# Encoder layer with attention: maxima issued by ScalarE, merged transfers, and a later store of the recurrence's outputs

## The reference, cut to what matters

```python
xn = rms_norm(x, norm_mix)
q, k, v, u, g_attn, g_ssm = jnp.split(xn @ w_in, SPLIT_POINTS, axis=-1)
q = apply_axial_rope(rms_norm(q.reshape(bsz, l, 16, 64), q_norm), cos, sin)
k = apply_axial_rope(rms_norm(k.reshape(bsz, l, 4, 64), k_norm), cos, sin)
attn_out = gqa_attention(q, k, v) @ w_attn_proj      # softmax(q k / 8) v, a kv head for 4 q heads
y = gelu(s5_bidirectional(u, ...))                   # a linear recurrence in both directions
ssm_out = (y @ w_glu_a) * sigmoid(y @ w_glu_b)
x = x + (sigmoid(g_attn) * attn_out + sigmoid(g_ssm) * ssm_out) @ w_out
x = x + square(relu(rms_norm(x, norm_mlp) @ w_ff1)) @ w_ff2
```

## Time and profile before

| what | value |
|---|---|
| time, median of three runs | 2325.09 us (2324.87 to 2328.51) |
| time of the profiled execution | 2325.24 us |
| its span in the trace | 2323.5 us |
| PE busy | 98% of the span |
| VectorE, ScalarE, GpSimd busy | 78%, 51%, 58% |
| TensorE clock granted, mean | 1.00 |

### The profile page before, as it was taken

One profiled execution on the slowest core, in us unless ns is written; L12 is line 12 of the kernel. 1 busy time (PEld: TensorE's weight loads), 2 busy tenths in 40 slices (PEclk: granted clock), 3 DMA queues, 4 the chain that ended last, 5 costly groups with the idle time before them and its releaser, 6 DMA issues.

```text
span 2323.5 us, 43966 instructions
## 1 busy us (share of the span) xinstructions
PE 2287.0 (98%) x14871; PEld 2000.0 (86%) x14871; DVE 1809.7 (78%) x2613; ACT 1192.4 (51%) x1980; POOL 1339.1 (58%) x1113
## 2 busy tenths in 40 slices
PE   8999999999989999999999999999999999999999
PEld 6888888888756666688888889999999999999999
DVE  6888578989878777867676698888888967777776
ACT  7556121121367777844444456555557465555563
POOL 0002864646457777744444446777777877667765
PEclk9999999999999999999999999999999999999999
DMA  5333344443333121165566654333333532222222
GB/s 195 114 125 119 116 122 110 116 123 108 109 89 101 47 60 37 39 205 177 185 201 200 212 176 136 97 97 97 97 98 106 191 128 73 73 73 73 73 73 91
DMA packets 173145, 271.01 MB, mean 117 GB/s; under 512 B 36529, under 2 KB 91057, under 8 KB 172849
## 3 DMA queue, kind: packets, MB, share of 16 engines
q1 hardware_dynamic: 172400, 268.62, 37.2%
q10 hardware_dynamic: 576, 0.27, 0.0%
HBM read 201.13 MB, written 57.67 MB: 111 GB/s over the span
## 4 chain that ended last, share of the span: by engine, by line
PE 89%; DVE 3%; SPq 3%; DMA 2%; ACT 2%; issue 1%; POOL 1%; ACTq 0%; DVEq 0%; POOLq 0%
PE banks L65 9%; PE banks L67 9%; PE banks L66 9%; PE banks L3237 6%; PE banks L3239 6%; PE banks L3240 6%; PE banks L3213 6%; PE banks L3215 6%; PE banks L3216 6%; PE p_acc L65 3%; PE p_acc L66 3%; PE p_acc L67 3%; PE banks L2095 3%; PE banks L2096 3%; PE banks L2064 2%; PE banks L2043 1%
## 5 line engine op out<-in xcount | busy, mean ns | idle before, releaser
L2707 POOL TENSOR_TENSOR t_wlo<-f_sums,t_whi 128x512 fp32r<-128x512 f32 x256 | 360.4, 1410 | 156.7 <-ACT t_whi L2738 156.7
L2995 DVE TENSOR_TENSOR f_x<-banks,f_x 128x384 f32<-128x384 f32 x448 | 245.1, 553 | 94.8 <-PE banks L3240 94.4
L1892 POOL TENSOR_TENSOR a_plo<-a_p 128x512 f16<-128x512 f32 x236 | 248.0, 1059 | 101.4 <-ACT a_p L1938 96.9
L2693 POOL TENSOR_TENSOR t_wlo<-t_wraw,t_whi 128x1024 fp32r<-128x1024 f32 x67 | 164.6, 2457 | 218.8 <-ACT t_whi L2723 218.8
L1938 ACT ACTIVATE a_p<-banks,s_scales 128x512 f32<-128x512 f32 x320 | 248.4, 778 | 82.2 <-PE banks L2096 56.9
L2738 ACT ACTIVATE t_whi<-f_sums 128x512 fp32r<-128x512 f32 x256 | 161.7, 632 | 230.9 <-PE banks L3240 147.1
L3213 PE MATMUL banks<-block,t_whi 128*128 128x384 f32 x720 | 241.7, 336 | 2.6 <-ACT stage L2852 1.5
L3216 PE MATMUL banks<-block,t_wlo 128*128 128x384 f32 x720 | 240.6, 334 | 0.0
L3215 PE MATMUL banks<-block,t_whi 128*128 128x384 f32 x704 | 235.3, 334 | 0.0
L1971 DVE TENSOR_REDUCE stage<-banks 128x1 f16<-128x1024 f32 (+1 forms) x184 | 191.0, 1058 | 43.9 <-PE banks L2064 42.9
L3237 PE MATMUL banks<-block,t_whi 128*128 128x384 f32 x608 | 203.4, 334 | 1.8 <-DVE f_x L2995 1.8
(11 more groups left out here) (428 smaller groups left out, 6840.0 us busy)
## 6 DMA issues: line engine op xcount, KB each, us to landing
t_wraw<-w_tail_t SPq DMA_DIRECT2D x136, 512.0 KB, 4.0
a_quotient<-w_tail_t SPq DMA_DIRECT2D x64, 512.0 KB, 3.8
w_raw<-w_in_t SPq DMA_DIRECT2D x31, 512.0 KB, 3.8
proj_scratch<-s_gate SPq DMA_DIRECT2D x48, 256.0 KB, 2.1
t_graw<-proj_scratch SPq DMA_DIRECT2D x24, 512.0 KB, 3.7
block<-roped_scratch SPq DMA_DIRECT2D x146, 64.0 KB, 2.2
p_sw<-p_qn SPq DMA_DIRECT2D x60, 128.0 KB, 2.1
mix_scratch<-a_quotient SPq DMA_DIRECT2D x48, 128.0 KB, 2.4
```

Of the source, the lines that this page charges most:

```text
L1892: pool.tensor_tensor(p_lo[s][:], p32[s][:], p_hi[s], ALU.subtract).then_inc(plo_pool, 1)
L2707: pool.tensor_tensor(weights_of(t, ring_lo[t % 4]), source(t), f32(weights_of(t, ring_hi[t % 4])), ALU.subtract).then_inc(lo_pool.sem, 1)
```

## The change

1. `place_max` goes from SP to ScalarE, right behind the first exponential of a unit, and places the maxima of the next unit. SP's unit begins with the wait for the scores. PE waits for the maxima between the two score matmuls of the unit's first step, and for the queries of the unit two ahead before the first matmul of its maxima.
2. `roped_scratch` is laid out as `[head, half, 64, tokens]` and no longer `[half, head, 64, tokens]`. The query loads are two DMAs for a unit and no longer three: high and low half as 128 rows into `q1`, and the high half into `q2`. The first keys are loaded by one DMA for each head, whose source is broadcast over the two halves of `k1`, in place of two DMAs for all heads asked for. The stores of `r_hi` and `r_lo` stay one DMA each, with a DRAM side of `[2, 64, 512]`.
3. The store of a pair's outputs is one DMA of 128 rows with a DRAM side of `[2, 64, 512]`, and no longer two of 64 rows; so too in the tail.
4. The stores of the recurrence's last outputs move from A's iterations g 0 and 2 to B's first four iterations, g 0 and 3. The first loads from `mix_scratch` for the next stage move from B's iterations 0 and 1 to B's iteration 4.

```diff
@@ -173,14 +173,14 @@
-        for rows in (0, HEAD):
-            sp.dma_start(self.k1[rows:rows + HEAD, h0:h1, tok],
-                         roped[0, NQ + h0:NQ + h1, :, tok].rearrange("h d n -> d h n")
+        for h in range(h0, h1):
+            sp.dma_start(self.k1[:, h, tok],
+                         roped[NQ + h, 0, :, tok].unsqueeze(0).broadcast_to([2, HEAD, tok.stop - tok.start])
                          ).then_inc(landed, 16)
...
         sp.dma_start(self.k2[0:HEAD, h0:h1, tok],
-                     roped[1, NQ + h0:NQ + h1, :, tok].rearrange("h d n -> d h n")).then_inc(self.k_in[n], 16)
+                     roped[NQ + h0:NQ + h1, 1, :, tok].rearrange("h d n -> d h n")).then_inc(self.k_in[n], 16)
@@ -198,10 +198,9 @@
         tok = bass.ds(blk * BLK, BLK)
-        hi, lo = roped[0][head][:, tok], roped[1][head][:, tok]
-        sp.dma_start(self.q1[kv][0:HEAD], hi).then_inc(self.q_in[kv], 16)
-        sp.dma_start(self.q1[kv][HEAD:P], lo).then_inc(self.q_in[kv], 16)
-        sp.dma_start(self.q2[kv][0:HEAD], hi).then_inc(self.q_in[kv], 16)
+        both = roped[head].rearrange("t d n -> (t d) n")
+        sp.dma_start(self.q1[kv], both[:, tok]).then_inc(self.q_in[kv], 16)
+        sp.dma_start(self.q2[kv][0:HEAD], both[0:HEAD, tok]).then_inc(self.q_in[kv], 16)
@@ -559,9 +558,7 @@
                 head = 4 * i + (2 * (t // NBLK) - (4 if k < 0 else 0))
-                return bass.ds(head * HEAD, P), cols(t % NBLK)
-
-            rows_of = lambda l: roped[l].rearrange("h d n -> (h d) n")
+                return bass.ds(head, 2), cols(t % NBLK)
@@ -577,11 +574,11 @@
                     if has(i, k, behind, own):
-                        rows, tok = place(i, k)
+                        heads, tok = place(i, k)
                         sp.wait_ge(hi_ready, 6 * i + (k + 1))
-                        sp.dma_start(rows_of(0)[rows, tok], r_hi[:, k % 2]).then_inc(hi_out[k % 2], 16)
+                        sp.dma_start(roped[heads, 0, :, tok], r_hi[:, k % 2]).then_inc(hi_out[k % 2], 16)
                         sp.wait_ge(lo_ready, 6 * i + (k + 1))
-                        sp.dma_start(rows_of(1)[rows, tok], r_lo[:, k % 2]).then_inc(lo_out[k % 2], 16)
+                        sp.dma_start(roped[heads, 1, :, tok], r_lo[:, k % 2]).then_inc(lo_out[k % 2], 16)
                 if behind and not own:
@@ -1639,12 +1636,12 @@
-                pe.wait_ge(mid.k_head_in, 32)
+                pe.wait_ge(mid.k_head_in, 16)
                 pe.wait_ge(resp_ready, BATCHES)
...
             def first_max(u_):
-                pe.wait_ge(mid.q_in[u_], 48)
+                pe.wait_ge(mid.q_in[u_], 32)
                 for j in range(4):
@@ -1656,7 +1653,7 @@
             outputs(Batch(None, BATCHES - 1), range(BATCH // 2))
-            pe.wait_ge(mid.k_first_in[0], 32)
+            pe.wait_ge(mid.k_first_in[0], 16 * (NKV - 1))
             first_max(1)
@@ -1804,9 +1801,8 @@
                 sp.wait_ge(moved, pair + 2)
-                for half in range(2):
-                    sp.dma_start(mix[head + NKV * half][:, bass.ds(blk * BLK, BLK)],
-                                 o[t][half * HEAD:(half + 1) * HEAD]).then_inc(stored[t], 16)
+                sp.dma_start(mix[bass.ds(head, 2, NKV), :, bass.ds(blk * BLK, BLK)],
+                             o[t][:]).then_inc(stored[t], 16)
@@ -1815,8 +1811,6 @@
-                if g % 2 == 0:
-                    store_outputs(sp, mix_y, last_y, slice(GROUPS - BATCH, GROUPS), st.y, (2 * g + kv,))
                 if g == 1:
@@ -1825,16 +1819,21 @@
-            def last_stage(g, kv):
-
-                if g == 0 and kv == 0:
+            def outputs_out(g, kv):
+
+                if g in (0, 3):
+                    store_outputs(sp, mix_y, last_y, slice(GROUPS - BATCH, GROUPS), st.y, (kv + (4 if g else 0),))
+
+            def last_stage(kv):
+
+                if kv == 0:
                     sp.wait_ge(pv_done, QKP + B.s0)
...
                     for s in range(2):
-                        sp.wait_ge(stored[s], 32 * (NQ // 4))
-                if g == 0 or kv < 2:
-                    fore.load_first(sp, mix_t, kv if g == 0 else 4 + kv)
+                        sp.wait_ge(stored[s], 16 * (NQ // 4))
+                for c in (kv, 4 + kv)[:2 if kv < 2 else 1]:
+                    fore.load_first(sp, mix_t, c)
             for sq in SEQS:
@@ -1844,9 +1843,6 @@
                         for kv in range(NKV):
-                            u = sq.u0 + it * 4 + kv
-                            if next_seq(sq, last, kv):
-                                mid.place_max(sp, u + 2, (kv + 2) % 4)
                             sp.wait_ge(scored, sq.s0 + sq.n * (it * 4 + kv + 1))
@@ -1862,7 +1858,9 @@
                             elif bi == 0 and isinstance(g, int):
-                                last_stage(g, kv)
+                                outputs_out(g, kv)
+                            elif bi == 1 and isinstance(g, int) and g == 0:
+                                last_stage(kv)
@@ -1924,7 +1922,7 @@
                 if not isinstance(before, int) or before:
-                    act.wait_ge(stored[t], 32 * before)
+                    act.wait_ge(stored[t], 16 * before)
                 act.activation(o[t][:], ps[:, O_BANK + 1], ACT.Copy, scale=mid.v_unscale[:, t:t + 1]).then_inc(moved, 1)
@@ -1937,6 +1935,10 @@
                                            scale=mid.score_scale).then_inc(exp_done, 1)
+                            first_of_all = sq is A and isinstance(it, int) and it == 0 and kv == 0
+                            last_of_all = sq is B and last and kv == NKV - 1
+                            if kt == 0 and not first_of_all and not last_of_all:
+                                mid.place_max(act, it * 4 + (sq.u0 + kv + 1), (kv + 1) % NKV)
                             i = v_part(V_SPLIT, sq, it, kv, kt)
@@ -2077,12 +2079,9 @@
-                        pe.wait_ge(nmax_in[kv], n_of(kv) * 16)
-                        pe.wait_ge(q_in[kv], n_of(kv) * 48)
+                        pe.wait_ge(q_in[kv], n_of(kv) * 32)
                         if sq_ahead is not sq and sq_ahead:
-                            pe.wait_ge(k_first_in[1], 32 * NKV)
-                        if sq_ahead:
-                            pe.wait_ge(q_in[s_ahead], n_of(kv + 2) * 48)
+                            pe.wait_ge(k_first_in[1], 16 * NKV)
                         for kt in range(sq.n):
@@ -2093,6 +2092,8 @@
                             pe.matmul(out, k1[:, kv, keys], q1[kv][:], start=True, stop=False)
+                            if kt == 0:
+                                pe.wait_ge(nmax_in[kv], n_of(kv) * 16)
                             pe.matmul(out, k2[:, kv, keys], q2[kv][:], start=False,
@@ -2110,6 +2111,8 @@
                             if sq_ahead:
+                                if kt == 0:
+                                    pe.wait_ge(q_in[s_ahead], n_of(kv + 2) * 32)
                                 for part in range(sq_ahead.n // sq.n):
@@ -2500,10 +2503,9 @@
                 sp.dma_start(ones[:], ones_d).then_inc(const_in, 16)
-                for half in range(2):
-                    sp.dma_start(mix[0:8].rearrange("t p n -> (t p) n").rearrange("(h d) n -> h d n", d=HEAD)
-                                 [NQ - 1 - NKV * (1 - half)][:, TOK - BLK:TOK],
-                                 fore.o[t_last][half * HEAD:(half + 1) * HEAD]).then_inc(st.attention[t_last], 16)
+                sp.dma_start(mix[0:8].rearrange("t p n -> (t p) n").rearrange("(h d) n -> h d n", d=HEAD)
+                             [bass.ds(NQ - 1 - NKV, 2, NKV), :, TOK - BLK:TOK],
+                             fore.o[t_last][:]).then_inc(st.attention[t_last], 16)
@@ -2620,7 +2622,7 @@
                     for s in range(2):
-                        sp.wait_ge(st.attention[s], 32 * (NQ * NBLK // 4))
+                        sp.wait_ge(st.attention[s], 16 * (NQ * NBLK // 4))
                     mix_chunk(b + 1, 0)
@@ -2764,7 +2766,7 @@
                         act.wait_ge(fore.turned, LAST_PAIR + 3)
-                        act.wait_ge(st.attention[t_last], 32 * (LAST_PAIR // 2))
+                        act.wait_ge(st.attention[t_last], 16 * (LAST_PAIR // 2))
                         act.activation(fore.o[t_last], ps[:, LAST_BANK], ACT.Copy,
@@ -3245,7 +3247,7 @@
     proj = scratch("proj_scratch", [PROJ_T, P, TOK])
-    roped = nc.dram_tensor("roped_scratch", [2, NQ + NKV, HEAD, TOK], F16).ap()
+    roped = nc.dram_tensor("roped_scratch", [NQ + NKV, 2, HEAD, TOK], F16).ap()
     mix = scratch("mix_scratch", [12, P, TOK])
```

## The result

The changed kernel takes 2373.66 us (median of four runs, 2371.75 to 2374.79), the kernel before on the same chip 2325.89: the ratio is 1.0203, with an interval of 1.0185 to 1.0220. The forecast was 2370, with 2338 to 2404 as its range. The span of the profiled execution is 2373.0 us, 49.5 more than before.

The account below looks back on a forecast made before the run. PE, busy 98% of the span, bounds the kernel; its waits for queries in A could be won. From 2325.24: -15.3 +2.0 +0.8 +0.5 +2.5 +27 (first projection) +27 (A) +1 (tail) = 2371, stated as 2370, range 2338 to 2404.

Parts of the forecast that it names:

- A: Attention of sequence A (512 keys): 27 us of new waits for queries, against 15.3 us gained, with small costs on top.
- The narrow transfers: Roped stores, first key loads, pair stores: an outermost count of 2 confines each to the same two DMA engines.
- Rival 2: All merged transfers: a count of 2 doesn't narrow them, so only the first part's gain remains, 2313; chance 0.13 with rival 4.
- Rival 3: Pair stores in A: at 8.2 us each fills a pair of units, seven more waits of about 3.5 us, 2395; chance 0.12.
- First projection: First projection: narrow roped stores slow VectorE until PE loses 27 us (18 to 38).
- the period of a tile: First projection: stores, swap and weights on two engines take 7.0 us a tile (6.7 to 7.4), against PE's 5.95.
- The cushion of 8.6 us: First projection: tile 39's low weights are ready at 235.1, PE starts it at 243.8; this lead is subtracted from 35 us.
- Rival 1: First projection hides the narrow stores, through several engine pairs or 24 GB/s per engine with the cushion holding: 2343; chance 0.08.
- Ahead of A: Start of A: three narrow key loads of 2.95 us stand ahead of unit 1's queries, costing 2.5 us.
- the walk: A's 15 units, with 5.6 us per store or key load and 0.6 for queries: waits at units 5 to 15, 27 us.
- The gain under it: A: maxima on ScalarE, two query loads and a later wait remove all 12 query waits, 15.3 us, before small costs.
- the signs that I named: First projection: DMA share 0.12 to 0.2, waits for VectorE and `p_sw`; longer landings; A's longest waits at units 7 and 9.

Follow-up runs that it names:

- the probe: Separate program of single transfers, each waited for, without the layer; 128 KB took 4.84 us with outermost count 2, 1.73 us with 128 rows.
- keys_halves: The changed kernel with only the first keys as transfers of 64 rows, roped and pair stores left narrow: 2357.87 us, ratio 1.0134.
- before_maxima: The kernel before, with only the maxima issued by ScalarE and PE's waits moved; layout and transfers as they were: 2317.95 us, ratio 0.9961.
- mix_halves: The changed kernel with only the pair-output store as two transfers of 64 rows, roped stores and first keys left narrow: 2347.64 us, ratio 1.0089.

## Why the prediction was right

**The narrow transfers.** Two engines for an outermost count of 2, all on the same pair: shown by the probe. By the Trainium skill, page DMA: Bandwidth & Descriptors, section on why a DMA increments its semaphore by 16, the count of 2 gives two engines, always the lowest-numbered; the busy share of 0.13 for one store and 0.14 for two agrees with two engines shared by all. Which two they are, no view here tells. So the trace's one case (L1182) carried to the case that it didn't show. Rival 2 (2313, faster) is what happens when they are made wide: 2314.34. 128 rows in one transfer take 1.73 us in the probe, two halves 2.62, a narrow one 4.84. So the advice on the same page of the Trainium skill (rules for authors), one transfer of 128 partitions in place of two halves, agrees with the probe where the other side isn't split and fails where it is split in two; there another of its rules, that an outermost count under 16 confines a transfer to as many engines, decides.

**Rival 3, slow stores.** It put the drain of a narrow pair store at 8.2 us, the forecast at 5.6. In the probe the narrow one takes 5.7 us longer than the wide one (7.69 and 2.00); with 0.7 for the drain of that on 16 engines (an eighth of 5.6) it is 6.4, nearer to the forecast.

**First projection: right mechanism, price too high.** 27 us forecast, 17.8 measured. The term that was too large is the period of a tile, 7.0 us. PE's waits for the means stand at 141.06, 161.04, 180.97, 201.00 and 220.91, 19.96 apart for three tiles, so 6.65; the last tiles come faster, and VectorE evicts tile 33 at 252.37. That is 23 us late and not 35. Behind the period stands the drain of a roped store, 2.95 us at 21 to 22 GB/s per engine: in the window shown it is 49 GB/s on two engines, 24.5 each, so 2.67. (The prediction's 2.8 "at the best rate seen" doesn't follow from its rows either: 25.2 GB/s gives 2.6.) The cushion of 8.6 us, by which the low weights of a tile were ready before PE started it, was right. The low weights of tile 39, which PE started at 243.77 before the change, are ready at 258.68 + 1.26 = 259.94, 24.8 us later than before, and PE starts the tile right behind them:

```profile
258.68 1.26 DVE L798 TENSOR_TENSOR w_lo<-w_raw,w_hi 128x1024 fp32r<-128x1024 f32 x1 [0.26 <-ACT w_hi L611]
...
260.04 0.76 PE L65 MATMUL p_acc<-block,w_hi 128*128 128x512 f32 x1 [2.74 <-issue]
```

So PE is 16.3 us late there, and 24.8 less the cushion is 16.2. How PE lost them doesn't matter to the sum: 11.2 us are its waits (8.5 + 2.7), the rest slower matmuls, at a clock of 0.89 from 215 to 230 us, and small pieces. The other 1.5 us come behind that point and were not in the sum: PE's clock is at its lower level for a part of tile 39 (0.76 us for this first matmul, where 0.39 is usual; 0.90 from 260 to 275). Rival 1 is out: the rate was the one it asked for, but the cushion didn't hold against 24.8 us.

**Ahead of A: too low.** 2.5 forecast, 6.3 measured: the keys hold PE for 3.6 us, and then the clock is low (the four matmuls of first_max take 1.87 us, before 1.03; the granted clock over the 24 us ahead of A is 0.86). When they start, PE has lost 3.4 us since the end of the first projection; from there to the first scores it loses 2.9 more.

**A: the waits right in sum, not in kind; the clock missed.** The forecast had 27 us of waits, all for queries. There were 17.5 for queries and 10.3 for maxima, 27.8. The largest two are at units 7 and 9 as I had walked them, 6.4 and 5.5 us, each behind 1.9 and 1.8 for maxima. By unit the waits are 3.2, 8.3, 7.3, 3.1, 3.1 and 2.8 us at 5, 7, 9, 11, 13 and 15, where the walk had 1.5, 8, 7.5, 2, 2.5 and 2.5; the 1.5 that it had at 8 and at 10 didn't come. Too little at the odd units and too much at the even ones cancel in the sum. The term that was left out is the clock: 9.2 us. That is about the whole difference of 23.8 to 14.5. The gain under it was sized right in sum: with wide transfers A is 11.7 us shorter (12.5 forecast), though I had ascribed it to SP's order and the query load alone. Those two gave 10.2, and 1.5 is the later stores of the recurrence, which I had priced at nothing.

**What was luck.** 2370 against 2373.66 hides a miss of 9 in the first projection and of 13 behind it, of opposite signs. Of the signs that I named, one was wrong and one came in another form. Wrong was the fall of the DMA engines' busy share to 0.12 to 0.2 over the first projection. It stayed at 0.34 (0.36 before). The same packets take the same engine time in nearly the same span; only within single microseconds is the narrow pair seen (0.14). The landing of the narrow transfers couldn't be read. VectorE's wait for `p_sw` was as forecast: 39.5 us in 19 waits from 60 to 270 us, 4.0 before. But the row of PE's waits for the means names ScalarE (L688) and not VectorE. It is the same chain, one step on: ahead of the wait at 141.06 VectorE waited 3.12 us for `p_sw`, and ScalarE 4.72 us for VectorE's sum (L894).

## What to carry to other kernels

Write out the shape of both sides of a DMA as [outermost, ..., row] before merging two into one: if a merge puts a count of 2 outermost, the transfer may save an issue of 0.6 us and take longer by 2.2 us than its two halves (4.84 for 2.62, 128 KB) or by 5.7 us than with 128 rows (7.69 for 2.00, 256 KB). Such transfers queue on one pair of engines, so they hold up every other transfer that has a share there, also those of another engine's queue; look at the busy share in a window of one microsecond while one drains, since the average over a stage doesn't show it. When PE is made to wait for several microseconds at a time, or again and again for 1 to 2 us in close pairs, reckon with time on top of the waits for the clock: here a third to a half more in A (9.2 for 27.8, 8.8 for 18.7, 4.1 for 9.3).

## What the runs showed that I had not expected

The clock: before the change PE stood still 13.3 us in A, in 12 pieces of at most 2.0 us, at a granted clock of 1.00. With waits of 1.0 to 6.4 us in close pairs it is 0.88 over A, and the first matmul after the long one takes 0.61 us where 0.38 is usual; 0.88 is a mean over its two levels, 2.4 and 1.2 GHz. In keys_halves no wait in A is longer than 2.0 us either, but each wait for maxima has one for queries 1.5 to 2.0 us behind it, and the clock is 0.92. In before_maxima, with 3.9 us of waits for queries in A, it is 1.00.

An issue that doesn't come back: behind a narrow key load SP's issue of the queries took 3.1 to 4.5 us, four times. In A of mix_halves, where the pair stores are wide, the longest are 2.1 and 1.7 us, and in A of keys_halves, where the keys are wide, none is over 1.5. So in A stalls of over 3 us came only with the narrow store and the narrow key load together, and then SP's instruction stream stands still too. In the probe, where nothing is queued ahead, the issue takes 0.6 us. What holds it no run shows.

One narrow store of 128 KB alone moved 38 GB/s on its two engines, two at once 47 to 49, so two that overlap cost less than twice one. Between 16, 32, 64 and 128 rows outermost there is still a difference, 2.32, 2.11, 2.06 and 1.73 us. I looked for the cause of neither.
